# Two norms at the end of a two-block transformer, each done for 128 tokens at a time

## The reference, cut to what matters

```python
c = cross_attention(h, mem_n, w_cq, w_ckv, w_co)      # ends in a 1024x1024 product with w_co
x = x + rms_norm(c, g_post_cross)
h = rms_norm(x, g_pre_ffn)
gu = h @ w_gate_up                                     # 1024 x 5632
f = (silu(gu[..., :2816]) * gu[..., 2816:]) @ w_down   # 2816 x 1024
x = x + rms_norm(f, g_post_ffn)                        # the output
```

## Time and profile before

| | |
|---|---|
| median of 3 runs | 1443.86 us (1442.03 to 1444.58) |
| the profiled execution's own time | 1445.57 us |
| its span, first to last instruction | 1443.8 us |
| TensorE busy | 1419.3 us, 98% of the span |
| VectorE, ScalarE, GpSimd busy | 856.0, 692.2 and 209.0 us |
| mean granted TensorE clock | 0.993 of full speed |

### The profile page before, as it was taken

The page is one execution under the profiler, slowest core; times in us unless marked ns, Lnnn a source line. Parts: engine busy times, 40 slices in busy tenths (PEclk is TensorE's granted clock), DMA queues, the critical chain, the costliest instruction groups (busy, mean ns, idle before and its releaser), DMA issues.

```text
span 1443.8 us, 18478 instructions
## 1 busy us (share of the span) xinstructions
PE 1419.3 (98%) x7252; PEld 1200.6 (83%) x7252; DVE 856.0 (59%) x1007; ACT 692.2 (48%) x939; POOL 209.0 (14%) x416
## 2 busy tenths in 40 slices
PE   8999999999999999999999999999999999899997
PEld 6888889988888888888899888888887989788886
DVE  5555565856555565555667565555776665555554
ACT  6545355345444454444645464444554444444442
POOL 1000000002232122231022022221101100032230
PEclk9999999999999999999999999999999999899999
DMA  9755544455655656656444357656444543266651
GB/s 354 269 179 192 184 175 175 149 201 180 224 199 201 219 177 219 216 196 213 174 146 147 124 183 279 215 197 213 163 145 144 192 163 130 102 231 214 213 201 61
DMA packets 64183, 272.73 MB, mean 189 GB/s; under 512 B 14528, under 2 KB 30144, under 8 KB 33248
## 3 DMA queue, kind: packets, MB, share of 16 engines
q1 hardware_dynamic: 52512, 258.12, 50.2%
q0 software_dynamic: 11584, 13.42, 3.0%
HBM read 259.95 MB, written 1.05 MB: 181 GB/s over the span
## 4 chain that ended last, share of the span: by engine, by line
PE 95%; ACT 1%; DVE 1%; DMA 1%; SPq 1%; issue 0%; POOL 0%; POOLq 0%; DVEq 0%; ACTq 0%
PE prod L1067 16%; PE prod L1069 15%; PE prod L1068 15%; PE acc L1069 10%; PE acc L1067 10%; PE acc L1068 10%; PE prod L1061 4%; PE prod L1063 4%; PE prod L1062 4%; PE acc L1237 1%; PE acc L1084 1%; DMA raw<-in_weights_dram 1%; PE acc L1257 1%; ACT w_hi L1377 1%; PE aux L1097 0%; ACT acts_h L1395 0%
## 5 line engine op out<-in xcount | busy, mean ns | idle before, releaser
L1574 DVE TENSOR_TENSOR w_lo<-raw,w_hi 128x2048 fp32r<-128x2048 f32 x235 | 538.1, 2291 | 385.3 <-ACT w_hi L1377 385.0
L1377 ACT CAST w_hi<-raw 128x2048 fp32r<-128x2048 f32 x235 | 447.9, 1907 | 428.0 <-PE prod L1069 175.4
L1067 PE MATMUL prod<-w_hi,acts_h 128*128 128x512 f32 x944 | 373.0, 395 | 1.9 <-DVE w_lo L1582 0.7
L1069 PE MATMUL prod<-w_hi,acts_l 128*128 128x512 f32 x944 | 368.7, 391 | 0.0
L1068 PE MATMUL prod<-w_lo,acts_h 128*128 128x512 f32 x944 | 368.5, 390 | 0.0
L1067 PE MATMUL acc<-w_hi,mix_h 128*128 128x512 f32 x600 | 236.4, 394 | 0.0
L1069 PE MATMUL acc<-w_hi,mix_l 128*128 128x512 f32 x600 | 233.8, 390 | 0.0
L1068 PE MATMUL acc<-w_lo,mix_h 128*128 128x512 f32 x600 | 233.5, 389 | 0.0
L943 POOL DMA_DIRECT2D four<-four x320 | 157.0, 498 | 444.5 <-DVE four L1703 426.0
L1067 PEld LDWEIGHTS prod<-w_hi,acts_h 128*128 128x128 f32 x944 | 177.9, 188 | 43.8 <-issue 8.0
L1069 PEld LDWEIGHTS prod<-w_hi,acts_l 128*128 128x128 f32 x944 | 177.8, 188 | 37.4
(11 more groups left out here) (259 smaller groups left out, 1260.2 us busy)
## 6 DMA issues: line engine op xcount, KB each, us to landing
raw<-in_weights_dram SPq DMA_DIRECT2D x235, 1024.0 KB, 5.0
four<-four SPq DMA_DIRECT2D x320, 16.0 KB, 2.1
four<-four POOLq DMA_DIRECT2D x320, 16.0 KB, 1.8
raw<-in_weights_dram SPq DMA_DIRECT2D x12, 256.0 KB, 6.8
work<-in_mem_dram POOLq DMA_DIRECT2D x2, 1024.0 KB, 11.8
grow<-in_gain_rows_dram POOLq DMA_DIRECT2D x4, 512.0 KB, 4.2
tabs<-in_tabs_dram POOLq DMA_DIRECT2D x1, 1696.0 KB, 8.9
work<-in_x_t_dram SPq DMA_DIRECT2D x4, 256.0 KB, 5.6
```

The lines of the kernel that those rows point to most:

```text
L1067: pe.matmul(out, still_hi, wh, start=first, stop=False, skip_group_check=True)
L1069: return pe.matmul(out, still_lo, wh, start=False, stop=last, skip_group_check=True)
L1377: act.copy(w_hi[:, c % RING], raw[:, c % RAW]).then_inc(hi_done, 1)
L1574: dve.tensor_tensor(w_lo[:, c % RING], raw[:, c % RAW], w_hi[:, c % RING].bitcast(F32), ALU.subtract).then_inc(lo_done, 1)
```

## The change

The last two output norms are done for tokens 0 to 127 first and tokens 128 to 255 after. The last chunk of `w_co` and of `w_down` finishes the banks in the order 0, 2, 1, 3. GpSimd makes two statistics of one column each, and the gain row's DMA comes after the second. VectorE adds the first token half as soon as its `rstd` is there; TensorE transposes that half (all 1024 features), ScalarE copies it in eight pieces of 128x128 and VectorE makes the low part in as many. TensorE runs U1 and U2 for t = 0, with the transposes of the second token half between them, and then U1 and U2 for t = 1. ScalarE runs a one-element Silu ahead of those copies, and copies U3's weights between the two token halves; U4's weights are copied after the first pair's two Silu instead of before them, on VectorE likewise. At the end, the adds and the stores go by token half too.

```diff
 class Plan
+    def post_halves(self, gain):
+        self.last_down["by_tokens"] = True
+        self.add("post_sums", gain=gain, y=self.y, y_chunk=self.y_chunk, n=self.stat, y_copied=self.y_copied,
+                 halves=True)
...
+        for half in range(2):
+            self.add("stat", n=self.stat, of="y", slot="y", half=half)
+            self.stat += 1
+    def prep_halves(self, gain):
+        self.add("prep_halves", gain=gain, first=self.acts, acts_free=self.acts_users, x_new=self.x_new,
+                 x_turned=self.x_turned, n=self.stat, y_copied=self.y_copied - 4)
...
+        self.early_half = True
+        self.statistic("x", "x")
     def up(self, source, p):
-                       acts=self.acts, free=self.bank_free(2))
+                       acts=self.acts, free=self.bank_free(2), early_half=self.early_half)
...
+        self.early_half = False
 make_plan
+BY_TOKENS = (0, 2, 1, 3)
-    pl.post_norm("g_post_cross")
-    pl.prep("g_pre_ffn", "post")
+    pl.post_halves("g_post_cross")
+    pl.prep_halves("g_pre_ffn")
     pl.ffn("w_gate_up_2", "w_down_2", 0)
-    pl.post_norm("g_post_ffn")
-    pl.add("store", x_new=pl.x_new)
+    pl.post_halves("g_post_ffn")
+    pl.add("store", x_new=pl.x_new, y_copied=pl.y_copied - 4, n=pl.stat)
 SyncE: the four stores
-            for b in range(4):
+            for n, b in enumerate(BY_TOKENS):
                 t, cols = piece(b)
-                sp.wait_ge(x_new, first + b + 1)
+                sp.wait_ge(x_new, first + n + 1)
 GpSimd: statistic() on columns t = half:half+1 instead of both, and
-                    if next_row:
+                    if next_row and it.get("half") != 0:
                         done, count, row = next_row
                         pool.wait_ge(done, count)
                         pool.dma_start(grow[:], A["gain_rows"][row]).then_inc(gain_row_loaded, 16)
 TensorE
+            def turn_tokens(it, t):
+                pe.wait_ge(x_new, it["x_new"] + 2 * t + 2)
+                for b in (t, t + 2):
+                    for i in range(4):
+                        kt = 4 * (b // 2) + i
+                        mm = pe.transpose(acc[b][:, tokens(i)], x[:, t, kt * P:(kt + 1) * P], ident)
+                    mm.then_inc(x_turned, 1)
 (tokens_chunk)
-                        if seen[of] < it["acts"] and t == 0:
+                        if it.get("early_half") and t == 0:
+                            pe.wait_ge(early_lo, kt + 1)
+                        elif seen[of] < it["acts"] and (t == 0 or it.get("early_half")):
                             pe.wait_ge(lo_done_of, it["acts"] - KT + kt + 1)
 (down_chunk)
+                order = BY_TOKENS if it.get("by_tokens") else range(4)
+                for n, b in [(n, order[n]) for part in parts for n in (2 * part, 2 * part + 1)]:
 (main loop)
+                elif kind == "up" and it["early_half"]:
+                    chunk(it, (0,))
+                    late_half.append(it)
+                    if it["k_half"]:
+                        for late in late_half:
+                            chunk(late, (1,))
+                elif kind == "prep_halves":
+                    turn_tokens(it, 0)
+                    pending.append((it, 1))
 ScalarE
                 elif kind in ("up", "cols", "rows_half", "down", "group"):
-                    flush()
+                    if kind != "up" or not it["early_half"]:
+                        flush()
...
                             act.activation(gate_s[:, t], up_bank(it, t)[:, 0:S], ACT.Silu,
                                            scale=rstd["x"][:, t:t + 1]).then_inc(silu_done, 1)
+                        if it["early_half"]:
+                            flush()
+                elif kind == "prep_halves":
+                    flush(state["target"] - 1)
+                    act.wait_ge(chunk_used, it["acts_free"])
+                    act.wait_ge(acts_lo, it["first"])
+                    act.activation(head_stats[:, it["n"] % 4, 8:9], vecs[:, 0:1], ACT.Silu)
+                    for t in range(2):
+                        for b in (t, t + 2):
+                            act.wait_ge(x_turned, it["x_turned"] + 2 * t + b // 2 + 1)
+                            for i in range(4):
+                                kt = 4 * (b // 2) + i
+                                act.activation(acts_h[:, kt, tokens(t)], acc[b][:, tokens(i)], ACT.Copy,
+                                               scale=gain_col(it["gain"], kt)).then_inc(acts_hi if t else early_hi, 1)
+                        for b in (t, t + 2):
+                            ins = square(x[:, t, piece(b)[1]], b, it["n"])
+                        if t == 0:
+                            flush()
+                    ins.then_inc(squared, 1)
 VectorE
+            def scaled_output(it, n):
+                b = BY_TOKENS[n]
+                t, cols = piece(b)
+                dve.wait_ge(y_squared, it["y_copied"] + n + 1)
+                dve.tensor_tensor(ybuf[:, t, cols], acc[b], grow[:, cols], ALU.mult).then_inc(y_copied, 1)
+            def add_half(it, t):
+                dve.wait_ge(rstd_done, it["n"] - 1 + t)
+                dve.wait_ge(y_copied, it["y_copied"] + 2 * t + 2)
+                for b in (t, t + 2):
+                    cols = piece(b)[1]
+                    dve.scalar_tensor_tensor(out=x[:, t, cols], in0=ybuf[:, t, cols], scalar=rstd["y"][:, t:t + 1],
+                                             in1=x[:, t, cols], op0=ALU.mult, op1=ALU.add).then_inc(x_new, 1)
+            def lo_half(it, t, k, hi_done_of, first, lo_done_of):
+                dve.wait_ge(hi_done_of, first + 4 * k + 4)
+                for i in range(4):
+                    kt = 4 * k + i
+                    dve.scalar_tensor_tensor(out=acts_l[:, kt, tokens(t)], in0=acc[t + 2 * k][:, tokens(i)],
+                                             scalar=gain_col(it["gain"], kt),
+                                             in1=acts_h[:, kt, tokens(t)].bitcast(F32), op0=ALU.mult,
+                                             op1=ALU.subtract).then_inc(lo_done_of, 1)
 (up)
+                    early = kind == "up" and it["early_half"]
+                    if not early:
+                        flush(state["target"] - 1 if kind == "down" and it["turn"] else None)
...
                         if m in plan.moves:
                             dve.wait_ge(mid_done, 2 * m + 2)
                             dve.transpose(mid_blocks, four[:, 1, :]).then_inc(blocks_turned, 1)
+                        if early:
+                            flush()
+                elif kind == "prep_halves":
+                    for n in range(2):
+                        scaled_output(it, n)
+                    add_half(it, 0)
+                    scaled_output(it, 2)
+                    lo_half(it, 0, 0, early_hi, 0, early_lo)
+                    scaled_output(it, 3)
+                    lo_half(it, 0, 1, early_hi, 0, early_lo)
+                    add_half(it, 1)
+                    flush(state["target"] - 1)
+                    for k in range(2):
+                        lo_half(it, 1, k, acts_hi, it["first"], acts_lo)
+                    flush()
                 elif kind == "store":
-                    dve.wait_ge(rstd_done, plan.stat)
-                    for b in range(4):
...
+                    for n in range(3):
+                        scaled_output(it, n)
+                    add_half(it, 0)
+                    scaled_output(it, 3)
+                    add_half(it, 1)
```

More of the change, by code:

```diff
@@ L211, in post_norm @@
     def post_norm(self, gain):
-        self.add("post_sums", gain=gain, y=self.y, y_chunk=self.y_chunk, n=self.stat, y_copied=self.y_copied)
+        self.add("post_sums", gain=gain, y=self.y, y_chunk=self.y_chunk, n=self.stat, y_copied=self.y_copied,
+                 halves=False)
         self.y_copied += 4
@@ L992, in statistic @@
                 n, r = it["n"], rstd[it["slot"]]
+                t = slice(0, 2) if it.get("half") is None else slice(it["half"], it["half"] + 1)
                 if it["of"] == "y":
@@ L1086, in turn_half @@
                     mm.then_inc(x_turned, 1)
+            def turn_tokens(it, t):
[5 more added lines that the diff above has]
+                    mm.then_inc(x_turned, 1)
             def turn_pending():
                 while pending:
-                    turn_half(*pending.pop(0))
+                    it, half = pending.pop(0)
+                    if it["kind"] == "prep_halves":
+                        turn_tokens(it, half)
+                    else:
+                        turn_half(it, half)
             def turn_mid(it):
@@ L1149, in down_chunk @@
                         pe.wait_ge(mid_done, 4)
-                    for n, tile in enumerate(it["tiles"]):
-                        mm = token_passes(acc[b], slot, n * D + 512 * (b // 2), mix_h[:, tile, tokens(t)],
-                                          mix_l[:, tile, tokens(t)], it["first"] and n == 0, it["last"] and n == 1)
```

(30 more changed lines are left out.)

28 lines of the change are left out of this document (20 added, 8 removed).

## The result

| | median | against before, 95% interval |
|---|---|---|
| before, 20 runs beside the changed kernel | 1443.49 us | |
| after, 20 runs | 1446.31 us | 1.0016 [1.001, 1.0022] |

The change made the kernel slower by about 2.3 us by the ratio (0.16% of 1444; 2.8 by the medians), which is under the 2.9 us that were taken as no change. The forecast was 1443.9; the median lies 2.4 above it and 0.1 above the top of the range. The profiled execution of after took 1446.4 us, with a span of 1444.6.

What follows compares the result with a forecast made beforehand. TensorE was taken as the bound, holding 95% of the chain. Terms of -0.1 at U5, +1.5 for the clock and -1.4 at the end summed to 0.0, put on the median: 1443.9 us, range 1439.5 to 1446.2.

Steps and rivals of the forecast that it cites:

- Front gain: Norm behind cross-attention through the first pair: second Silu moves from 1265.26 to 1262.4, 2.9 us gained.
- The table: ScalarE ahead of the first copies: the Silu table load of 1.28 us is hidden, with 0.5 to spare.
- The rival by the Trainium skill's page: Silu table load ahead of the copies: a 1380 ns drain besides, +0.8 us, 1444.7; 2 in 100.
- What is late next: SP's queue: first pair's moves wait behind D0's DMA and U4's low part, making U5 2.8 us later, giving back 2.9.
- U5: Start of U5's matmuls: 1276.25 against 1276.31, a change of -0.1 us.
- Clock behind U5: TensorE behind its 2.8 us wait ahead of U5: a slow stretch costs 0 to 2.56 us, taken as 1.5.
- The end: Last norm: two adds instead of four follow the last `rstd`, 1.37 us gained (bounds 0.7 to 1.4).
- the forecast of no change: Whole kernel: difference under 0.2% (2.9 us), given 71 in 100.
- The first rival: At U5: moves land in time, front gain stays, no slow clock behind it: -4.3 us, 1439.6; 17 in 100.

Runs made afterwards that it cites:

- copy_back: The changed kernel with U4's copy and low part ahead of pair 0's Silu and products again: 1444.02 us, 1.0007 against the kernel before.
- the three runs with the same code: Kernel before, its code kept up to the last norm, with only the end altered: 1446.53, 1443.77 and 1441.08 us.
- no_dummy: The changed kernel without the one-element Silu, so the Silu table loads ahead of the first pair's first Silu: 1444.85 us, 1.0012 against the kernel before.
- moves_first: The changed kernel with SyncE issuing pair 0's eight moves ahead of D0's transfer: 1441.47 us, 0.9986 against the kernel before.
- the two mends together: The changed kernel, pair 0's moves ahead of D0's transfer, last norm's statistics on ScalarE and VectorE instead of GpSimd: 1439.16 us, 0.9967 against before.
- late_pool: The kernel before plus one small GpSimd memset behind the output's last add, which nothing waits for: 1446.53 us, 1.002.
- tail_dve: The kernel before with only the last norm by halves, its statistics on VectorE and ScalarE instead of GpSimd: 1441.08 us, 0.998.

## Why the prediction was right, and where it was not

- **Front gain**, forecast 2.9 us up to the second Silu, measured 2.36. Transposes came 1.96 earlier (forecast 2.0). Eight 128x128 copies took 2.17, so one every 0.27, against the 0.3 taken, and the first dense matmul gained 2.25 instead of 1.8. From there to the second Silu it was 14.85 instead of 13.9: the clock was at 0.50 for all of the first twelve. The prediction added 1.5 to 12.4 here, with bounds of 1.1 and 2.56; the trace added 2.45. Where the clock held (copy_back: 1248.17 to 1261.14) it was 12.97, so the clock cost 1.9 in this execution.
- **The baseline.** The 2.36 is taken against a slow execution of before, and so was the forecast: it took the 14.96 from U1 to the second Silu, and the 2.56 of the clock in it, from the one profile. In the three runs with the same code that stretch was 13.75 to 13.87. Against them, a front with a slow clock after the change gains 1.2, and one with a held clock 3.0 (no_dummy: 17.05 behind the square).
- **The table** was hidden, as forecast; no_dummy agrees. The rival by the Trainium skill's page is out. "ScalarE: Activation LUTs", section "What ACT_TABLE_LOAD costs", counts 1380 ns of drain beside the load; here the one-element Silu starts 0.01 us behind the load's end, and the trace doesn't agree.
- **What is late next**: right, and shown from both sides. Moving the copy alone into the kernel before makes U5 3.0 us late; freeing the moves alone takes the wait away. SyncE's first move came 5.05 us behind the second Silu (forecast 5.0), the blocks 7.11 behind that (6.8), U5 2.04 behind them (2.05).
- **U5**, forecast -0.1, measured +0.79: 0.54 from the front gain and 0.35 from the steps behind it, the landing above all. The mechanism was right, the terms a little short. The landing's share is no more than scatter: from SyncE's first move to the copy it was 7.02 to 7.64 in the three runs with before's code. Against these runs U5 is 1.5 to 2.0 late. In no_dummy, where the clock held, it stands at 31.05, as early as theirs: there the front's gain is given back and no more.
- **Clock behind U5**, forecast +1.5, measured +1.62 in the profile, and 1.4 to 1.6 in the three profiles in which it fell. It is a chance and not a rule: no_dummy's profile had nearly the same wait (3.15 against 3.37) and lost nothing.
- **The end**, forecast -1.4, measured +0.25. This is the step that failed: "two adds follow instead of four: 1.37 gained". The adds did come 1.1 earlier and the stores were through earlier; but the last store already was not what ended the program. GpSimd's drain did, 1.2 us behind SyncE (1443.5 against 1442.3), in the kernel before as well. It begins with the last statistic, and that came no earlier by halves: its first instruction took 0.66 instead of 0.19, in all six profiles with this end, beside the adds that the change had moved forward.

So the forecast of no change held because the front's gain was given back where and how it was said. That it held by its number is in part luck. The three misses have one sign, they nearly fill the 2.9 us that counted as no change, and the range was made wide for the clock and not for the end, where the largest miss was. Its sum, 0.0, was 2.66 short of the two profiles: 1.65 at the end, 0.89 at U5, 0.12 for the clock. The first rival, in which the front gain stays, is the run moves_first; it gave -2.0 and not -4.3, mostly for the same missing end (1.65); its U5 came 2.43 earlier than in the profile of before, and not 2.9.

## What to carry to other kernels

When a step is moved behind another, follow not only who reads its result but whose queue waits for it: here U4's copy had time in hand for TensorE, and a DMA queue that waited for its low part held eight small transfers of another pair. Putting it back in front of the products only moved the wait; reordering the queue removed it. Before shortening the end of a kernel, read which engine is through last at the line where all of them meet, and not only the chain of work: the two mends together took 4.8 us from the kernel before, where the change alone added 2.3. And read the profile of before beside others of the same code: here the one that was used had a slow stretch at the very place that the change touches, and 1.2 us of the gain read from it was not the change's.

## What was not expected of the hardware

- GpSimd's drain at the program's end lasts 6.6 us from the end of its last instruction, in the profile before (1436.91 to 1443.5), after (1437.74 to 1444.4) and in late_pool (1437.67 to 1444.3). In tail_dve it starts 34 us ahead of the end, takes 7.49, and is hidden. ScalarE's was 0.7 and SyncE's 0.007.
- The trace put SyncE's last wait down to TensorE's queue, whose drain had long been over (1431.2 + 4.3 in after).
- The clock of one and the same kernel differs from run to run: over the span 0.994 to 0.998 in the changed kernel. Its time is shorter where the clock is higher, 1442.7 us on average at 0.998 (two runs) and 1447.0 at 0.995 or less (12 runs). Waits of 1.67, 1.35 and 3.15 us at U1 and U5 stand in a profile without any slow stretch ahead of the end (no_dummy), and waits of 1.67, 1.27 and 3.37 in one with two (after).
- GpSimd's small statistic instructions take longer beside some of VectorE's. Of the 34 on L1027 and L1031 in after, 23 took 0.18 to 0.21 us. The other 11 took 0.57 to 2.10, and each ended 0.05 or 0.06 behind the end of a subtraction for a low part or of a residual add on VectorE: 2.10 us until 1257.96 beside one that ended at 1257.91, and the one above, 0.66 us until 1436.84, beside an add that ended at 1436.79. That the one holds up the other is what this suggests; no run tests it.
